# RMS norms of a two-layer prompt and decode step on one core: sums of squares by token, the inverse root spread by a product with the identity

## Chip, cores, metric

The kernel runs on one core of one Trainium2 chip, as a single launch. The metric is the device time of that launch in microseconds, the median of several runs.

## What is computed

The reference runs a trunk of two layers over 256 prompt tokens and 8 x 4 sampled tokens, 1024 features wide, all in float32. Each layer has a mixer and a feed-forward part, and each part stands between two RMS norms, so there are eight norms with 1024 features:

```python
def rms_norm(x, g):
    xf = x.astype(F32)
    y = xf * lax.rsqrt(jnp.mean(xf * xf, axis=-1, keepdims=True) + EPS)
    return (y * g.astype(F32)).astype(x.dtype)

# per layer; sh, sc, gt come from cs @ w_ada + b_ada
h = modulate(rms_norm(x, g_pre_mix), sh1, sc1)      # h * (1 + scale) + shift
x = x + gt1 * rms_norm(mixer(h), g_post_mix)
h = modulate(rms_norm(x, g_pre_ffn), sh2, sc2)
x = x + gt2 * rms_norm(ffn(h), g_post_ffn)
```

Layer 0's mixer is latent attention beside dilated attention, its feed-forward part a dense SwiGLU of width 2816. Layer 1's mixer is windowed attention with sinks, its feed-forward part eight SwiGLU experts of width 3584, two to a token.

## The kernel before, in words

All activations stand transposed: features over the 128 partitions, in eight blocks k of 128 features, and tokens along the row, 288 of them (0 to 255 prompt, 256 to 287 sampled). So `xT`, `hT`, `fT` and `sq` are each 128 x 8 x 288. PSUM has eight banks of 512 columns: `bank(i, n, at)`. Each engine has its own written-out program, and they meet at semaphores; the order of work on an engine is the order of its code. A float32 product is two passes on TensorE, and the trace has a row for each weight load and each matmul of a pass ("x2" is one product); a transpose is one pass.

Norms are numbered 0 to 7: even ones are the pre-norms, odd ones the post-norms. Each goes through four engine steps:

- Squares. ScalarE squares each block into `sq[:, k, :]`, from PSUM, from `xT` (`x_squares`) or from `fT`.
- Sums over features, in `sums(n)` of TensorE. For norm 0 and the odd norms VectorE has added the eight blocks first (`add_square`, L1864) and one product of `ones` (128 x 128, stationary) with `sq[:, 0, :]` (288 columns) gives the sums, the same on all partitions (L691). For norms 2, 4 and 6 there are eight such products, one as each block of squares arrives (L695; in `sums_and_late` L1095).
- Root: ScalarE, `std(n)`, Sqrt of 128 x 288 from bank 7 into `rstd`. Inverse: VectorE, a reciprocal of 128 x 288 from `rstd` to `rinv` in SBUF (L1849 in `pre_norm`, L1885 in `post_norm`).
- Use. `post_norm` multiplies each of eight blocks of `fT` by `rinv` (L1890) and adds it to `xT` (L1897), and each finished block releases the next norm's square. `pre_norm` multiplies the sampled tokens (L1850, L1851), then the eight blocks of the prompt (L1853), and ScalarE adds the shift to each (`add_shift`); each finished block of `hT` releases products of the next linear layer.

In layer 0 norms 1 and 2, and 3 and 4, run in `sums_and_late(n, j0)`: TensorE has three further tasks there, `late_rows` of the second layer's modulation (L1073). One task is eight blocks k of two products, each 32 stationary columns with 256 moving ones, so 32 passes. Before the change TensorE's order is: task 0, blocks 0 to 2; `sums(n)`; task 0, blocks 3 to 7; task 1, blocks 0 to 3; then the eight sums of norm n+1 with task 1's blocks 4 to 7 after sums 0, 2, 4 and 6; then the whole of task 2; then the next linear layer (L1187 feed-forward, or L1208 for the projections of layer 1). Norms 5 and 6 (layer 1) have no such tasks beside them: after norm 6 TensorE runs the router (L1238, moving operand 8 columns wide), transposes (L1246) and the counting products of the routing (L1251, L1254), then the experts. Norm 0's sums are made at the start, and its root waits until the modulation of layer 0 is ready; before its use TensorE turns the weights `kvb` (L791). Norm 7 ends the kernel: its output blocks are turned by 24 transposes (L1455) into banks 0 to 5, copied and stored.

The weight transfers are issued by SyncE in a fixed order, each as soon as the products that used its ring slot are done.

Of the kernel before, what the change touches and what calls it, by code (L numbers as in the profile page):

```python
# [18 lines left out]
ALU = mybir.AluOpType  # L19
ACT = mybir.ActivationFunctionType  # L20
AX_X = mybir.AxisListType.X

D, P, KD = 1024, 128, 8
NTP, NB, TS = 256, 8, 4
NS = NB * TS
NT = NTP + NS
# [33 lines left out]
C_EPS = C_CM + 128  # L60
# [111 lines left out]
def build(nc, t_in, t_out):  # L172
# [12 lines left out]
    with ctx:  # L185
        def sb(name, shape, dt=F32):
            return ctx.enter_context(nc.sbuf_tensor(name, shape, dt))

        def sem(name):
            return ctx.enter_context(nc.semaphore(name))  # L190
# [4 lines left out]
        xT = sb("xT", [P, KD, NT])  # L195
# [2 lines left out]
        o_or_q = sb("o_or_q", [P, KD * NT])  # L198
        rinv_rstd = sb("rinv_rstd", [P, 2 * NT])
        rinv, rstd = rinv_rstd[:, 0:NT], rinv_rstd[:, NT:2 * NT]  # L200
        mod = sb("mod", [P, 2, 48, 9])
        coef = sb("coef", [P, 4, KD, 9])
        cst = sb("cst", [P, NCST])
# [17 lines left out]
        fT = work[:, 2304:4608].rearrange("p (k n) -> p k n", k=KD)  # L221
        sq = work[:, 4608:6912].rearrange("p (k n) -> p k n", k=KD)
# [74 lines left out]
        htok = [work[:, 4608:4608 + D], work[:, 4608 + D:4608 + 2 * D], o_or_q[:, 0:D]]  # L297
        pick = o_or_q[:, D:D + 3 * PICK].rearrange("p (t n) -> p t n", t=3)
        E_BANK = ((0, 1, 2, 1), (3, 1, 2, 1))
        G_BANK = (0, 1, 2)  # L300
        logit = rt[:, 0:24].rearrange("p (t n) -> p t n", t=3)
        top = rt[:, 24:48].rearrange("p (t n) -> p t n", t=3)
        topi = rt[:, 48:72].bitcast(U32).rearrange("p (t n) -> p t n", t=3)
# [16 lines left out]
        def bank(i, n=512, at_=0, rows=P):  # L320
            return ps[0:rows, 512 * i + at_:512 * i + at_ + n]

        ident = cst[:, C_ID:C_ID + 128]
        ones = cst[:, C_ONE:C_ONE + 128]
# [8 lines left out]
        sq_done, sq_added, stat_done, std_done = sem("squares_done"), sem("squares_added"), sem("sums_done"), sem("std_done")  # L333
# [22 lines left out]
        chain_v = sem("vector_chain")  # L356
# [11 lines left out]
        e_ptp, e_pcp = sem("put_transposed"), sem("put_copied")  # L368
        chain_e = sem("vector_chain_experts")

        rest_zero = sem("rest_rows_cleared")
        k_used, s_kr = sem("key_tile_used"), sem("rope_keys_loaded")
        s_new, s_ncp = sem("new_token_scores_done"), sem("new_token_scores_copied")
# [307 lines left out]
        def _(pe):  # L681
# [5 lines left out]
            def sums(n):  # L687

                if n % 2 or n == 0:
                    pe.wait_ge(sq_added, (n + 1) // 2 + 1)  # L690
                    mm(bank(7, NT), ones, sq[:, 0, :], start=True, stop=True).then_inc(stat_done, 1)  # L691
                    return
                for k in range(KD):
                    pe.wait_ge(sq_done, 8 * n + k + 1)
                    last = mm(bank(7, NT), ones, sq[:, k, :], start=(k == 0), stop=(k == KD - 1))  # L695
                last.then_inc(stat_done, 1)

            def ada_rows(w, b, before_last=None):

# [87 lines left out]
            for hp in range(4):  # L787
# [3 lines left out]
                    last = tp(bank(b, 128, 128 * q, 64), kvb[:, c, 128 * h:128 * h + 64], ident)  # L791
                last.then_inc(t_done, 1)
                nt += 1


            def sample_rows(b, x, w, width, k, nk):

# [265 lines left out]
            def late_rows(j, k0, k1):  # L1063

                if k0 == 0:
                    landed("ada1", j)
                    if j % 3 == 0:
                        pe.wait_ge(ada_add, 12 + j)
                w = chunk("ada1", j, 0, 4096).rearrange("p (k m) -> p k m", k=KD)
                r0, c0 = 64 * (j % 3 // 2), 3072 + WA * (j % 3 % 2)  # L1070
                for k in range(k0, k1):
                    for g in range(NT_ADA):
                        last = mm(ps[r0 + CB * g:r0 + CB * g + CB, c0:c0 + WA], csT[:, k, :], w[:, k, WA * g:WA * g + WA],  # L1073
                                  start=(k == 0), stop=(k == KD - 1))
                if k1 == KD:
                    last.then_inc(ada_done, 1)
# [10 lines left out]
            def sums_and_late(n, j0):  # L1087

                late_rows(j0, 0, 3)
                sums(n)  # L1090
                late_rows(j0, 3, KD)
                late_rows(j0 + 1, 0, 4)
                for k in range(KD):
                    pe.wait_ge(sq_done, 8 * (n + 1) + k + 1)
                    last = mm(bank(7, NT), ones, sq[:, k, :], start=(k == 0), stop=(k == KD - 1))  # L1095
                    if k == KD - 1:
                        last.then_inc(stat_done, 1)
                    elif k % 2 == 0:
                        late_rows(j0 + 1, 4 + k // 2, 5 + k // 2)
                late_rows(j0 + 2, 0, KD)  # L1100

            def attention0():

# [124 lines left out]
            linear_out(2, "out_c", 4, KD, oT)  # L1228
            mm(bank(3, 4), ident, ones[:, 0:4], start=True, stop=True).then_inc(e_o, 2)
            sums(5)  # L1230
            sums(6)


            for t, (t0, n) in enumerate(TILES):
# [212 lines left out]
                    pass_body(NE * p_, p_)  # L1447
            pe.wait_ge(e_add, 64 * npass + 2)
            sums(7)

            for kk in range(2):
                pe.wait_ge(x_upd, 24 + 4 * kk + 4)
                for t, (t0, n) in enumerate(TILES):
                    for k in range(4):
                        last = tp(bank(3 * kk + t, 128, 128 * k, n), xT[:, 4 * kk + k, t0:t0 + n], ident)  # L1455
                    last.then_inc(y_tp, 1)


# [1 line left out]
        def _(act):  # L1460
            def fn(out, in_, f, **kw):
                return nc.scalar.activation(out, in_, f, **kw)  # L1462
# [3 lines left out]

            def std(n):
                act.wait_ge(stat_done, n + 1)
                fn(rstd[:, :], bank(7, NT), ACT.Sqrt, scale=1.0 / D, bias=cst[:, C_EPS:C_EPS + 1]).then_inc(std_done, 1)

            def add_shift(n, l, w):

# [342 lines left out]
            for i in range(6):  # L1815
                kk, t = i // 3, i % 3
                n = TILES[t][1]
                act.wait_ge(y_tp, i + 1)
                fn(htok[t][0:n, 512 * kk:512 * kk + 512], bank(i, 512, 0, n), ACT.Copy).then_inc(y_cp, 1)


        @block.vector
        def _(dve):
# [3 lines left out]
            def link(ins):  # L1827

                nv[0] += 1
                ins.then_inc(chain_v, 1)  # L1830
                dve.wait_ge(chain_v, nv[0])
# [8 lines left out]
            def pre_norm(n, l, w):  # L1840

                sh = mod[:, l, 24 * w:24 * w + 8, :]
                if n:
                    dve.wait_ge(x_upd, 4 * n)
                else:
                    dve.wait_ge(x_cp, KD)
                link(V.tensor_tensor(sample(hT), sample(xT), per_batch(coef[:, 2 * w, :, :]), ALU.mult))
                dve.wait_ge(std_done, n + 1)
                link(V.reciprocal(rinv[:, :], rstd[:, :]))  # L1849
                link(V.tensor_tensor(sample(hT), sample(hT), sample_rinv(), ALU.mult))  # L1850
                V.tensor_tensor(sample(hT), sample(hT), per_batch(sh), ALU.add).then_inc(h_part, 1)  # L1851
                for k in range(KD):
                    V.scalar_tensor_tensor(out=hT[:, k, 0:NTP], in0=xT[:, k, 0:NTP], scalar=coef[:, 2 * w, k, 0:1],  # L1853
                                           in1=rinv[:, 0:NTP], op0=ALU.mult, op1=ALU.mult).then_inc(h_part, 1)

            def sample_rinv():
                return rinv[:, NTP:NT].rearrange("p (b t) -> p b t", t=TS).unsqueeze(1).broadcast_to([P, KD, NB, TS])

            def add_square(n, k):

# [9 lines left out]
            def post_norm(n, m, w):  # L1870

                g = coef[:, 2 * w + 1, :, :]
                for k in range(KD):
                    if m == 3:
                        dve.wait_ge(sq_done, 8 * n + k + 1)
                    else:
                        dve.wait_ge(f_cp, 8 * m + k + 1)
                    add_square(n, k)
                    V.tensor_scalar(fT[:, k, 0:NTP], fT[:, k, 0:NTP], g[:, k, 0:1], None, ALU.mult)
                    last = V.tensor_tensor(fT[:, k, NTP:NT].rearrange("p (b t) -> p b t", t=TS),  # L1880
                                           fT[:, k, NTP:NT].rearrange("p (b t) -> p b t", t=TS),
                                           g[:, k, 1:9].unsqueeze(2).broadcast_to([P, NB, TS]), ALU.mult)
                link(last)
                dve.wait_ge(std_done, n + 1)
                link(V.reciprocal(rinv[:, :], rstd[:, :]))  # L1885
                base = nv[0]

                def scaled(k):
                    nv[0] += 1
                    V.tensor_tensor(fT[:, k, :], fT[:, k, :], rinv[:, :], ALU.mult).then_inc(chain_v, 1)  # L1890

                scaled(0)
                for k in range(KD):
                    if k + 1 < KD:
                        scaled(k + 1)
                    dve.wait_ge(chain_v, base + k + 1)
                    V.tensor_tensor(xT[:, k, :], xT[:, k, :], fT[:, k, :], ALU.add).then_inc(x_upd, 1)  # L1897
# [482 lines left out]
```

## Time and profile before

| | |
|---|---|
| time, median of 3 runs | 2053.6 us |
| lowest and highest | 2045.3 and 2057.38 us |
| the profiled execution: its own time | 2053.35 us |
| its span, first to last instruction | 2051.7 us |
| mean granted TensorE clock | 0.952 |
| busy: TensorE matmuls, weight loads, VectorE, ScalarE | 1832.5, 1356.3, 418.9, 334.2 us |
| DMA | 504.36 MB, mean 246 GB/s |

The rows come from that one execution. PE is TensorE's matmuls, PEld its weight loads, DVE VectorE, ACT ScalarE, SPq the transfer queue of SyncE; times are from the span's start. The granted clock is a share of 2.4 GHz: 1.00 is that level, 0.50 is 1.2 GHz. A mean over a stretch with both levels lies between.

### The profile page before, as it was taken

The numbers are of one execution on the slowest core, as the hardware profiler recorded it, in microseconds if no ns is written. First come the engines' busy times: TensorE is split into PE (matmuls) and PEld (weight loads), VectorE is DVE, ScalarE is ACT, GpSimd is POOL, SyncE is SP. The second block draws the span as 40 slices with busy tenths as digits, with TensorE's granted clock in tenths as the row PEclk, the third lists the DMA queues.
The fourth block names the chain that finished last, engine by engine and source line by source line (L and its number), as shares of the span: only waits on it lengthen the run. The fifth ranks groups of instructions, "written<-read, shape, count | busy, mean of one in ns | idle before, by whom it ended". The sixth has DMA issues, their size and how long they took to land.

```text
span 2051.7 us, 30167 instructions
## 1 busy us (share of the span) xinstructions
PE 1832.5 (89%) x12873; PEld 1356.3 (66%) x12874; DVE 418.9 (20%) x1260; ACT 334.2 (16%) x1000; POOL 53.3 (3%) x99
## 2 busy tenths in 40 slices
PE   6799898899999998988998979899989799988874
PEld 3455565667777745767997636399965499953532
DVE  1104333340000034642101211111012111021113
ACT  2122333230000023621100101000001010010102
POOL 1002120000000000000000000000000000000000
PEclk9998999799999997988999999999999999999997
DMA  9933857354334563051785999997749977869991
GB/s 350 363 127 115 275 212 259 111 176 156 123 98 128 166 212 81 32 214 64 275 320 206 370 398 387 402 358 267 281 164 395 394 278 302 314 231 402 386 401 40
DMA packets 252027, 504.36 MB, mean 246 GB/s; under 512 B 6953, under 2 KB 65497, under 8 KB 251746
## 3 DMA queue, kind: packets, MB, share of 16 engines
q1 hardware_dynamic: 248066, 495.49, 67.0%
q0 software_dynamic: 3808, 6.61, 1.1%
q8 instruction: 123, 2.02, 0.4%
q14 instruction: 30, 0.25, 0.0%
HBM read 499.05 MB, written 3.02 MB: 245 GB/s over the span
## 4 chain that ended last, share of the span: by engine, by line
PE 72%; DMA 12%; SPq 7%; issue 4%; DVE 3%; ACT 1%; POOL 0%; DVEq 0%
PE ps L1315 15%; PE ps L1297 8%; PE ps L1187 8%; PE ps L1365 8%; PE ps L755 7%; DMA big<-in_w_moe_out 6%; SPq L585 4%; DMA big<-in_w_ada 3%; PE ps L815 3%; PE ps L1262 3%; PE ps L1208 2%; DMA big<-in_w_moe_in 2%; PE ps L704 1%; DMA big<-in_cache_b_v 1%; SPq L539 1%
## 5 line engine op out<-in xcount | busy, mean ns | idle before, releaser
L1315 PE MATMUL ps<-big 128*128 128x128 f32 (+1 forms) x2688 | 316.2, 281 | 15.5 <-issue 15.5
L1315 PEld LDWEIGHTS ps<-big 128*128 128x128 f32 x2688 | 314.9, 194 | 16.8 <-issue 16.8
L1297 PE MATMUL ps<-big 128*64 128x256 f32 x2240 | 263.3, 393 | 45.4 <-issue 35.3
L1297 PEld LDWEIGHTS ps<-big 128*64 128x64 f32 x2240 | 163.9, 142 | 134.3 <-issue 52.5
L1187 PE MATMUL ps<-work,big 128*128 128x288 f32 x704 | 171.2, 406 | 1.0 <-ACT work L1462 1.0
L1462 ACT ACTIVATE gqkv<-ps 128x144 f32<-128x144 f32 (+1 forms) x231 | 66.6, 315 | 628.5 <-PE ps L1315 307.7
L2302 DVE TENSOR_TENSOR z<-ps,gqkv 128x256 f32<-128x256 f32 x224 | 69.1, 334 | 468.9 <-ACT gqkv L1462 468.9
L1349 PE MATMUL ps<-big,z 128*64 128x512 f32 x560 | 127.7, 598 | 37.1 <-DMA big<-in_w_moe_out 35.6
L1187 PEld LDWEIGHTS ps<-work,big 128*128 128x128 f32 x704 | 133.6, 190 | 38.3 <-issue 1.5
L1365 PE MATMUL ps<-z,big 128*128 128x128 f32 (+1 forms) x1344 | 155.6, 279 | 2.3 <-issue 2.3
L1365 PEld LDWEIGHTS ps<-z,big 128*128 128x128 f32 x1344 | 155.1, 191 | 2.8 <-issue 2.8
L1462 ACT ACTIVATE z<-ps 128x288 f32<-128x288 f32 (+5 forms) x107 | 43.9, 426 | 574.7 <-PE ps L1349 158.6
L1349 PEld LDWEIGHTS ps<-big,z 128*64 128x64 f32 x560 | 37.8, 136 | 120.8 <-issue 62.3
L704 PE MATMUL ps<-big,csT 128*32 128x256 f32 x576 | 70.0, 399 | 20.2 <-DMA big<-in_w_ada 19.0
L755 PE MATMUL ps<-z,big 128*128 128x288 f32 x352 | 85.6, 406 | 1.0 <-DVE z L2181 1.0
L1462 ACT ACTIVATE big<-ps 128x384 f32<-128x384 f32 (+11 forms) x137 | 56.0, 433 | 165.8 <-PE ps L704 63.6
L755 PEld LDWEIGHTS ps<-z,big 128*128 128x128 f32 x352 | 66.8, 190 | 19.8 <-DVE z L2181 1.4
L1462 ACT ACTIVATE work<-ps 128x288 f32<-128x288 f32 (+4 forms) x104 | 38.3, 394 | 196.7 <-PE ps L755 137.5
L704 PEld LDWEIGHTS ps<-big,csT 128*32 128x32 f32 x576 | 35.5, 115 | 49.9 <-DMA big<-in_w_ada 14.8
L755 PE MATMUL ps<-o_or_q,big 128*128 128x288 f32 x256 | 65.4, 420 | 0.6 <-ACT o_or_q L1462 0.6
L815 PE MATMUL ps<-big,work 128*128 128x512 f32 (+2 forms) x160 | 62.2, 548 | 3.3 <-ACT work L1462 3.3
L2305 DVE COPY z<-ps 128x432 f32<-128x432 f32 x8 | 4.9, 608 | 291.1 <-PE ps L1365 148.1
(319 smaller groups left out, 1646.2 us busy)
## 6 DMA issues: line engine op xcount, KB each, us to landing
big<-in_w_moe_in SPq DMA_DIRECT2D x112, 2048.0 KB, 14.8
big<-in_w_moe_out SPq DMA_DIRECT2D x56, 2048.0 KB, 19.8
big<-in_w_ada SPq DMA_DIRECT2D x24, 2048.0 KB, 13.2
big<-in_w_ffd_in SPq DMA_DIRECT2D x22, 1024.0 KB, 7.6
big<-in_w_ffd_out SPq DMA_DIRECT2D x8, 1408.0 KB, 6.8
big<-in_cache_b_k SPq DMA_DIRECT2D x4, 2048.0 KB, 8.0
big<-in_cache_mla_ckv SPq DMA_DIRECT2D x64, 128.0 KB, 2.6
big<-in_cache_b_v SPq DMA_DIRECT2D x4, 2048.0 KB, 11.6
```

The costliest lines, as they stand in the source:

```text
L585: sp.dma_start(wslot(q).rearrange("p (f m) -> p f m", f=4), src).then_inc(e_in[q], 16)
L704: last = mm(ps[CB * g:CB * g + CB, 512 * b:512 * b + WA], csT[:, k, :], w[:, k, WA * g:WA * g + WA], start=(k == 0), stop=(k == KD - 1))
L755: last = mm(bank(4 + k % 2, NT), w[:, f, 128 * m:128 * m + 128], rhs[:, f, :], start=(f == 0), stop=(f == nk - 1))
L815: last = mm(bank(nz % 4, w), hT[:, k, t0:t0 + n], wt[:, k, :], start=(k == 0), stop=(k == KD - 1))
L1187: last = mm(bank(2 * (f % 2) + g, NT), w[:, g, k, 128 * fb:128 * fb + 128], hT[:, k, :], start=(k == 0), stop=(k == KD - 1))
L1262: last = mm(bank(G_BANK[k // 3], CAP, CAP * (k % 3)), htok[t][:, 128 * k:128 * k + 128], pick[:, t, 0:CAP], start=(t == 0), stop=(t == 2))
L1297: last = mm(ps[64 * a:64 * a + 64, 512 * b + 256 * g:512 * b + 256 * g + 256], hsel[:, k, 0:NARROW], w[:, k, 256 * a:256 * a + 256], start ...
L1315: last = mm(bank(b, cols, 256 * g), w[g][:, k, 128 * i:128 * i + 128], hsel[:, k, 0:cols], start=(k == 0), stop=(k == KD - 1))
L1349: last = mm(ps[64 * d:64 * d + 64, 512 * 5:512 * 6], actT[:, q, 128 * m + 64 * half:128 * m + 64 * half + 64], w[:, i, 512 * d:512 * d + 5 ...
L1365: last = mm(bank(5 + k // 3, cols, CAP * (k % 3)), w[:, i, 128 * k:128 * k + 128], act, start=(q == 0 and i == 0 and k % 3 == 0), stop=(q ...
L1462: return nc.scalar.activation(out, in_, f, **kw)
L2302: V.tensor_tensor(out, bank(b, w, 256), sil[i % 2][:, 0:w], ALU.mult).then_inc(e_act, 1)
```

## The change

The sums are made by token instead of spread over all partitions. `sq` is now the stationary operand, in three pieces of 128 tokens (from token 0, 128 and 160: the last two overlap), and one column of `ones` is moved: three products where there was one, whose results are three columns of bank 7, a token to a partition. Root and reciprocal work on 128 x 3 (`rcol`). Then `spread(n)` on TensorE makes three products: stationary a column of `rcol` repeated 128 times, moving the identity (128 columns); that puts the inverse of every token on all partitions of bank 2, columns 0 to 287. VectorE's uses (L1850, L1853, L1890) read bank 2 instead of `rinv`. In `sums_and_late` the two `spread` calls stand two blocks of late rows behind the sums they belong to: after block 4 of task 0, and after block 1 of task 2. For norm 0 `spread` stands behind the transposes of `kvb`. The last transposes go to banks 0, 1, 3, 4, 5, 6.

```diff
--- before.py
+++ after.py
@@ -198,6 +198,7 @@
         o_or_q = sb("o_or_q", [P, KD * NT])
         rinv_rstd = sb("rinv_rstd", [P, 2 * NT])
         rinv, rstd = rinv_rstd[:, 0:NT], rinv_rstd[:, NT:2 * NT]
+        rcol = sb("rcol", [P, 2, 3])
         mod = sb("mod", [P, 2, 48, 9])
         coef = sb("coef", [P, 4, KD, 9])
         cst = sb("cst", [P, NCST])
@@ -298,6 +299,7 @@
         pick = o_or_q[:, D:D + 3 * PICK].rearrange("p (t n) -> p t n", t=3)
         E_BANK = ((0, 1, 2, 1), (3, 1, 2, 1))
         G_BANK = (0, 1, 2)
+        Y_BANK = (0, 1, 3, 4, 5, 6)
         logit = rt[:, 0:24].rearrange("p (t n) -> p t n", t=3)
         top = rt[:, 24:48].rearrange("p (t n) -> p t n", t=3)
         topi = rt[:, 48:72].bitcast(U32).rearrange("p (t n) -> p t n", t=3)
@@ -368,6 +370,7 @@
         e_ptp, e_pcp = sem("put_transposed"), sem("put_copied")
         chain_e = sem("vector_chain_experts")
 
+        rc_rdy, rb_rdy = sem("inverse_root_by_token"), sem("inverse_root_spread")
         rest_zero = sem("rest_rows_cleared")
         k_used, s_kr = sem("key_tile_used"), sem("rope_keys_loaded")
         s_new, s_ncp = sem("new_token_scores_done"), sem("new_token_scores_copied")
@@ -688,12 +691,26 @@
 
                 if n % 2 or n == 0:
                     pe.wait_ge(sq_added, (n + 1) // 2 + 1)
-                    mm(bank(7, NT), ones, sq[:, 0, :], start=True, stop=True).then_inc(stat_done, 1)
+                    token_sums(0, 0, 0).then_inc(stat_done, 1)
                     return
                 for k in range(KD):
                     pe.wait_ge(sq_done, 8 * n + k + 1)
-                    last = mm(bank(7, NT), ones, sq[:, k, :], start=(k == 0), stop=(k == KD - 1))
+                    last = token_sums(k, 0, KD - 1)
                 last.then_inc(stat_done, 1)
+
+            def token_sums(k, first, end):
+
+                for t, t0 in enumerate((0, 128, 160)):
+                    last = mm(bank(7, 1, t), sq[:, k, t0:t0 + P], ones[:, 0:1], start=(k == first and t == 0), stop=(k == end),
+                              skip_group_check=True)
+                return last
+
+            def spread(n):
+
+                pe.wait_ge(rc_rdy, n + 1)
+                for t, t0 in enumerate((0, 128, 160)):
+                    last = mm(bank(2, P, t0), rcol[:, 1, t:t + 1].broadcast_to([P, P]), ident, start=True, stop=True)
+                last.then_inc(rb_rdy, 1)
 
             def ada_rows(w, b, before_last=None):
 
@@ -791,7 +808,7 @@
                     last = tp(bank(b, 128, 128 * q, 64), kvb[:, c, 128 * h:128 * h + 64], ident)
                 last.then_inc(t_done, 1)
                 nt += 1
-
+            spread(0)
 
             def sample_rows(b, x, w, width, k, nk):
 
@@ -1088,16 +1105,20 @@
 
                 late_rows(j0, 0, 3)
                 sums(n)
-                late_rows(j0, 3, KD)
+                late_rows(j0, 3, 5)
+                spread(n)
+                late_rows(j0, 5, KD)
                 late_rows(j0 + 1, 0, 4)
                 for k in range(KD):
                     pe.wait_ge(sq_done, 8 * (n + 1) + k + 1)
-                    last = mm(bank(7, NT), ones, sq[:, k, :], start=(k == 0), stop=(k == KD - 1))
+                    last = token_sums(k, 0, KD - 1)
                     if k == KD - 1:
                         last.then_inc(stat_done, 1)
                     elif k % 2 == 0:
                         late_rows(j0 + 1, 4 + k // 2, 5 + k // 2)
-                late_rows(j0 + 2, 0, KD)
+                late_rows(j0 + 2, 0, 2)
+                spread(n + 1)
+                late_rows(j0 + 2, 2, KD)
 
             def attention0():
 
@@ -1228,7 +1249,9 @@
             linear_out(2, "out_c", 4, KD, oT)
             mm(bank(3, 4), ident, ones[:, 0:4], start=True, stop=True).then_inc(e_o, 2)
             sums(5)
+            spread(5)
             sums(6)
+            spread(6)
 
 
             for t, (t0, n) in enumerate(TILES):
@@ -1447,12 +1470,13 @@
                     pass_body(NE * p_, p_)
             pe.wait_ge(e_add, 64 * npass + 2)
             sums(7)
+            spread(7)
 
             for kk in range(2):
                 pe.wait_ge(x_upd, 24 + 4 * kk + 4)
                 for t, (t0, n) in enumerate(TILES):
                     for k in range(4):
-                        last = tp(bank(3 * kk + t, 128, 128 * k, n), xT[:, 4 * kk + k, t0:t0 + n], ident)
+                        last = tp(bank(Y_BANK[3 * kk + t], 128, 128 * k, n), xT[:, 4 * kk + k, t0:t0 + n], ident)
                     last.then_inc(y_tp, 1)
 
 
@@ -1466,7 +1490,7 @@
 
             def std(n):
                 act.wait_ge(stat_done, n + 1)
-                fn(rstd[:, :], bank(7, NT), ACT.Sqrt, scale=1.0 / D, bias=cst[:, C_EPS:C_EPS + 1]).then_inc(std_done, 1)
+                fn(rcol[:, 0, :], bank(7, 3), ACT.Sqrt, scale=1.0 / D, bias=cst[:, C_EPS:C_EPS + 1]).then_inc(std_done, 1)
 
             def add_shift(n, l, w):
 
@@ -1816,7 +1840,7 @@
                 kk, t = i // 3, i % 3
                 n = TILES[t][1]
                 act.wait_ge(y_tp, i + 1)
-                fn(htok[t][0:n, 512 * kk:512 * kk + 512], bank(i, 512, 0, n), ACT.Copy).then_inc(y_cp, 1)
+                fn(htok[t][0:n, 512 * kk:512 * kk + 512], bank(Y_BANK[i], 512, 0, n), ACT.Copy).then_inc(y_cp, 1)
 
 
         @block.vector
@@ -1846,15 +1870,16 @@
                     dve.wait_ge(x_cp, KD)
                 link(V.tensor_tensor(sample(hT), sample(xT), per_batch(coef[:, 2 * w, :, :]), ALU.mult))
                 dve.wait_ge(std_done, n + 1)
-                link(V.reciprocal(rinv[:, :], rstd[:, :]))
+                V.reciprocal(rcol[:, 1, :], rcol[:, 0, :]).then_inc(rc_rdy, 1)
+                dve.wait_ge(rb_rdy, n + 1)
                 link(V.tensor_tensor(sample(hT), sample(hT), sample_rinv(), ALU.mult))
                 V.tensor_tensor(sample(hT), sample(hT), per_batch(sh), ALU.add).then_inc(h_part, 1)
                 for k in range(KD):
                     V.scalar_tensor_tensor(out=hT[:, k, 0:NTP], in0=xT[:, k, 0:NTP], scalar=coef[:, 2 * w, k, 0:1],
-                                           in1=rinv[:, 0:NTP], op0=ALU.mult, op1=ALU.mult).then_inc(h_part, 1)
+                                           in1=bank(2, NTP), op0=ALU.mult, op1=ALU.mult).then_inc(h_part, 1)
 
             def sample_rinv():
-                return rinv[:, NTP:NT].rearrange("p (b t) -> p b t", t=TS).unsqueeze(1).broadcast_to([P, KD, NB, TS])
+                return bank(2, NS, NTP).rearrange("p (b t) -> p b t", t=TS).unsqueeze(1).broadcast_to([P, KD, NB, TS])
 
             def add_square(n, k):
 
@@ -1882,12 +1907,13 @@
                                            g[:, k, 1:9].unsqueeze(2).broadcast_to([P, NB, TS]), ALU.mult)
                 link(last)
                 dve.wait_ge(std_done, n + 1)
-                link(V.reciprocal(rinv[:, :], rstd[:, :]))
+                V.reciprocal(rcol[:, 1, :], rcol[:, 0, :]).then_inc(rc_rdy, 1)
+                dve.wait_ge(rb_rdy, n + 1)
                 base = nv[0]
 
                 def scaled(k):
                     nv[0] += 1
-                    V.tensor_tensor(fT[:, k, :], fT[:, k, :], rinv[:, :], ALU.mult).then_inc(chain_v, 1)
+                    V.tensor_tensor(fT[:, k, :], fT[:, k, :], bank(2, NT), ALU.mult).then_inc(chain_v, 1)
 
                 scaled(0)
                 for k in range(KD):
```


## Rows read from the trace of the kernel before

**Rows 1.** The page, parts 1 and 2: busy time; granted clock by slices

```profile
...
PE 1832.5 (89%) x12873; PEld 1356.3 (66%) x12874; DVE 418.9 (20%) x1260; ACT 334.2 (16%) x1000; POOL 53.3 (3%) x99
...
PEclk9998999799999997988999999999999999999997
...
```

**Rows 2.** Chain of waits, 430 to 470 us: start us, us, what

```profile
...
441.34 0.70 PE ps L691 x2
...
442.06 0.51 ACT rinv_rstd L1462
...
442.66 1.96 DVE rinv_rstd L1885
...
446.37 0.75 PE ps L1095 x2
447.13 0.56 PE ps L1073 x4
447.68 1.17 PE ps L1095 x4
...
454.17 1.97 DVE rinv_rstd L1849
...
456.16 0.44 DVE work L1850
...
458.13 11.88 PE ps L1187 x48
...
```

**Rows 3.** Timeline, 430 to 460 us (start, us, engine, line): TensorE's runs of L1073

```profile
...
441.95 4.08 PE L1073 MATMUL ps<-big,csT 128*32 128x256 f32 x36
...
```

**Rows 4.** Windows: busy us of each engine, then granted clock, DMA share, GB/s

```profile
...
446.00:454.00 8.00, 7.66 (x40) 3.54 (x40) 5.06 (x14) 3.79 (x9) 0.00 (x0) 1.00 1.00 321
...
906.00:914.00 8.00, 7.19 (x16) 4.86 (x16) 5.17 (x14) 3.76 (x9) 0.00 (x0) 0.58 0.89 326
...
918.00:926.00 8.00, 7.84 (x48) 7.81 (x48) 6.36 (x15) 2.90 (x8) 0.00 (x0) 0.50 0.00 0
...
```

**Rows 5.** Timeline, 885 to 935 us: layer 1's norms and the router

```profile
...
906.48 7.19 PE L695 MATMUL ps<-work,cst 128*128 128x288 f32 x16 [4.35 <-ACT work L1462]
...
918.16 7.95 PE L1238 MATMUL ps<-wrout,work 128*128 128x8 f32 x48 [4.50 <-ACT work L1462]
...
931.00 1.40 PE L1251 MATMUL ps<-big,cst 128*128 128x8 f32 x12
...
933.10 0.21 ACT L1462 ACTIVATE big<-big 128x3 f32<-128x3 f32 x1
...
933.54 0.18 DVE L2243 RECIPROCAL big<-big 128x3 f32<-128x3 f32 x1
...
```

**Rows 6.** Timeline of TensorE, 368 to 400 us: products of 128 columns

```profile
...
381.89 0.79 PE L1034 MATMUL ps<-big,z 128*128 128x128 f32 x2 [0.58 <-ACT big L1462]
...
382.90 0.63 PE L1036 MATMUL ps<-big,z 128*128 128x128 f32 x2
...
398.19 0.49 PE L1034 MATMUL ps<-big,z 128*128 128x128 f32 x2
...
398.74 0.39 PE L1036 MATMUL ps<-big,z 128*128 128x128 f32 x2
...
```

**Rows 7.** Groups of VectorE by form, whole span: busy us, mean ns | idle

```profile
...
L2313 DVE TENSOR_TENSOR work<-ps,work 128x288 f32<-128x288 f32 x64 | 27.0, 454 | 7.1 <-PE ps L1395 4.5 <-PE ps L1393 0.8
...
L1890 DVE TENSOR_TENSOR work<-work,rinv_rstd 128x288 f32<-128x288 f32 x32 | 14.2, 453 | 0.1
...
L1849 DVE RECIPROCAL rinv_rstd<-rinv_rstd 128x288 f32<-128x288 f32 x4 | 7.8, 1954 | 9.3 <-ACT rinv_rstd L1462 9.3
...
```

**Rows 8.** Timeline, 86 to 104 us, around norm 0

```profile
...
88.45 1.91 PE L791 MATMUL ps<-cst,big 128*64 128x128 f32 x16 [0.52 <-DVE mod L1952]
...
89.72 1.95 DVE L1849 RECIPROCAL rinv_rstd<-rinv_rstd 128x288 f32<-128x288 f32 x1
...
```

**Rows 9.** Timeline, 2018 to 2051 us, norm 7

```profile
...
2026.52 1.30 PE L691 MATMUL ps<-work,cst 128*128 128x288 f32 x2 [7.83 <-DVE work L1864]
...
```

## Prediction

> **What bounds the kernel now.** I read the page first: TensorE's matmuls are busy 1832.5 us, 89% of the span, VectorE 20%, ScalarE 16%, and the clock digits are mostly 9 [rows 1]. So a microsecond counts where TensorE waits for a norm, or where a norm's own products stand in TensorE's way. Then the chain of waits around norms 1 and 2. Norm 1's sum starts at 441.34; the reciprocal of 128 x 288 lasts 1.96 us; TensorE takes up norm 2's sums at 446.37, the second reciprocal starts at 454.17, its result is used at 456.16, and the feed-forward products start at 458.13 [rows 2]. The chain has two characters. From 446.37 to 453.5 it lies wholly on TensorE, which alternates two sums (1.17) and one block of late rows (0.56): here TensorE's throughput is the bound, not the squares. Before and behind that, root, reciprocal and hops are the bound, while TensorE works off late rows, 36 passes in 4.08, 0.113 each [rows 3]; that leaves it idle for 0.34 before the first sum, and the 32 passes behind the last one end 1.0 before the feed-forward starts. Last the clock: in 446 to 454 TensorE has 1.00; in 906 to 914, after the idle time behind norm 5, it has 0.58 though busy for 7.19 of 8.00; and in 918 to 926, in the router, 0.50 although busy for 7.84 of 8.00 [rows 4].
>
> **The change part by part.** Prices first. Root of 128 x 3: 0.21, as the small ScalarE row; reciprocal of 128 x 3: 0.18; hops 0.04 to 0.10. A token sum is three weight loads of 128 x 128 in each of two passes, with one moving column: its nearest rows are L1251, six such products with 8 columns in 1.40, and the router, 24 products in 7.95 at the low clock, 16 of them 128 tokens wide and 8 of them 32 [rows 5]. L1251 gives 0.70 for three with their end; I take 0.66 in a stream and 0.80 alone. The router gives 0.33 a product if the narrow ones cost as much as the wide ones and 0.50 if they cost nothing, so 1.0 to 1.5 for three; I take 1.33, twice the full-clock value. A spread is three products with 128 moving columns: three such in a row span 398.19 to 399.13, 0.94, at full clock and 381.89 to 383.53, 1.64, at low clock [rows 6]. VectorE's 68 uses (4 of L1850, 32 each of L1853 and L1890) now read PSUM: 454 ns with a PSUM operand against 453 without [rows 7], so nothing; for L1853's form no row shows PSUM, and I bound it by 0 and by 0.02 each.
>
> A rule speaks against token sums, too. The Trainium skill, "TensorE: Matmul & The Clock Gate", section "LDWEIGHTS (loading the stationary operand)", gives a load as its columns over 1.2 GHz whatever the contraction: 107 ns for 128, an estimate of 0.64 for a token sum, and it names no slower clock. By it the router's loads would take 3.9 us; the row has 7.84 busy [rows 4], so the trace disagrees at the low clock. The sum would be near 2059 by that rule.
>
> Norm 1. Before: sum to first use 441.3 to 444.65, 3.35 us, with a root of 0.51 [rows 2]. After: sum 0.80, root 0.21, reciprocal 0.18, hops 0.25: ready at 442.7. TensorE has meanwhile taken two blocks of late rows (8 passes, 0.87) and comes to `spread` at 442.95, so the new wait on it costs nothing; use at 443.95, 0.7 earlier. That is worth nothing by itself: the squares come 0.7 earlier, but TensorE now has 0.9 more to do before it can take them, and its idle 0.34 is all that hides it. It starts the sums at 446.9 instead of 446.37. The loop of eight sums: a period was 1.17 + 0.56 = 1.73; now 2 x 0.66 + 0.43 (four passes of late rows) + 0.2 for the switches = 1.95. Loop 8.0 instead of 7.2. At full clock norm 2's sum is ready at 454.85, 1.3 late; root to use costs 1.8 (late-row blocks and spread included) instead of 2.6, so use 0.55 late; and TensorE, with spread among its 32 late passes, is free for the feed-forward at 459.3 instead of 458.13. So **+1.2** at full clock.
>
> But I don't expect full clock. In that loop 5.3 of 8.0 us would be weight loads with one column moved. The only stretch of such work in the trace, the router, kept 0.50 for all its 8 us with TensorE busy, and the clock came back only in the 128-column transposes behind it; the sums of 906 to 914, 288 columns wide, won it back within their own 7.2 us [rows 4, 5]. So the loop should lose the clock in its middle. With some 2.9 us of it left, that costs 2.9; the two late blocks 0.9 and the spread 0.7 more; of the 24 late passes behind it (2.7 us at full clock) I let a few run slow, 0.5 more, since wide work runs again from the end of the loop on. +1.2 + 2.9 + 0.9 + 0.7 + 0.5 = +6.2, taken as **+6**. Bounds: +1.2 with the clock kept, +10 if it is lost early in the loop and not back when the feed-forward starts. Norms 3 and 4 have the same code around them and, by the timeline, the same times to 0.1 us: **+6** again. The feed-forward and projection products behind them are TensorE's own throughput, so nothing takes it back; the weight transfers wait for slots that these free, and shift along.
>
> Norms 5 and 6. First use 0.9 earlier (3.4 less 2.45), no late rows. Sums of norm 6 from 905.6, at the low clock as now, 8 x 1.33 = 10.6 instead of 7.19: their end comes at 916.2, not 913.7. Root to use 2.4 with a low-clock spread (2.6 before): **+2.3**, and the router behind it is at the low clock in both. Nothing follows it but a chain of small steps, all of it shifted.
>
> Norm 0: TensorE is through L791 at 90.36; a spread of 0.94 gives 91.4, the reciprocal's end was 91.67 [rows 8]: **-0.3**. Norm 7, at the low clock: the sum took 1.30 [rows 9], now 1.45; root and reciprocal save 0.3 and 1.77, spread and a hop add 1.74: **-0.2**. New banks at the end, no new wait: 0.
>
> Sum: 6 + 6 + 2.3 - 0.3 - 0.2 = +13.8, against the profiled execution's own 2053.35 (span 2051.7 and 1.65 around it): 2067.2. That execution lies 0.25 below the median shown, so the same holds for the median. Since the clock may come back sooner in one of the pairs, I say 2066.
>
> **Rivals.** *The clock holds in both loops.* For it: the late rows between the sums, 256 columns, are no weight loads, and they had 1.00 among the wide sums. Against: the router. The time is 1.2 + 1.2 + 2.3 - 0.5 = +4.2, 2057.5: not slower by what a measurement can tell. The Trainium skill, same page, section "Part 1: The HAM clock gate (the \"warmup\" mystery)", says the gate goes by how busy the engine has recently been; by that rule the loop, busy throughout, would hold. The router, busy 7.84 of 8.00 at 0.50, contradicts it.
>
> *The spread fills norm 5's pause.* 0.94 us of products in the 5 us between norm 5's sum and norm 6's might keep the clock up. Then a token sum (0.66) keeps pace with the squares, which come a use and an add of VectorE apart (0.45 busy each, overlapping [rows 7]), norm 6 is used 3.6 earlier, and the router and what follows gain some 1.5 more. With held loops: 2.4 - 5.1 - 0.5 = -3.2, 2050. It decides only if the clock is still 1.00 at 905.6; in the rows of before it is 0.50 by 906, and one short burst is little against a pause of over 3 us. Faster by over 0.5% I can't build from any case.
>
> *The clock stays away longer.* If the low stretch reaches through both loops' tails into the linear layers, 10 each: +22, 2075.
>
> *It doesn't do what it says*: VectorE slower on PSUM or a reciprocal of three columns with a long fixed part. The rows above leave 2 us at most.
>
> **How the numbers follow.** 0.5% is 10.3 us, about what a measurement of this kernel can tell from no change (the three runs shown lie within 12 us). Forecast 0.62, clock held in the loops 0.22, spread fills the pause 0.06, clock away longer 0.10. The forecast lies 3 us above the bound, and one loop's bounds reach below it, so a fifth of it counts as no change. Slower 0.62 x 0.8 + 0.10 = 0.60; same 0.12 + 0.22 + 0.03 = 0.37; faster 0.03. Range: 2054 to 2076, from just under the held clock to the longer loss; the forecast alone 2061 to 2072.
>
> **What would show it.** Right: granted clock clearly under 1.00 in some part of 446 to 462 and of 723 to 739; the last sum of norms 2 and 4 four microseconds late; feed-forward and projections starting about 6 late; norm 6's sums lasting over 10 us; the uses of L1890 0.37 apart as before. Wrong: clock 1.00 through both loops, or norm 6's sums as fast as the squares arrive.

## The result and the profile after

The changed kernel takes 2058.94 us (median of 20 runs) where the kernel before takes 2052.35 (20 runs on the same chip): ratio 1.0033, 95% interval 1.0017 to 1.005, so +7 us, with an interval from +3 to +10. The profiled execution itself took 2050.91 us, less than the profiled one of before (2053.35): the two spans alone would call the change faster. So I read the stages, not the spans. (One of the 20 runs of the changed kernel, 2234.75 us at a mean granted clock of 0.813, is left out of the ratio, as are the two runs like it in the experiments, 2446.88 and 6385.98 us.)

The chain of waits of the changed kernel through norms 1 and 2, the counterpart of [rows 2] (start in us, length, engine, what, line, instructions); L704 is a pass of a token sum (x6 is one token sum: three products of two passes), L712 of a spread, L1090 of late rows, L1208 the feed-forward:

```profile
439.96 0.22 PE ps L704 x2
440.19 0.56 PE ps L1090 x4
440.74 1.43 PE ps L704 x12
442.17 0.87 PE ps L1090 x4
443.04 2.65 PE ps L704 x12
445.69 0.99 PE ps L1090 x4
446.68 1.37 PE ps L704 x6
448.05 1.85 PE ps L1090 x8
449.90 1.58 PE ps L712 x6
451.48 3.24 PE ps L1090 x24
454.72 15.47 PE ps L1208 x63
```

Two token sums (x12) take 1.43 in the first rows and 2.65 in the fifth; late rows go from 0.56 to 0.99. Nothing waits: the chain is TensorE's from end to end, where before it went over ScalarE and VectorE. Root and reciprocal have left it, and the clock has taken more than they gave. The windows say so [rows 4]: granted clock (the figure third from the end) of 1.00, then a mean of 0.77 and of 0.64, with TensorE busy throughout.

```profile
431.00:438.00 7.00, 7.00 (x62) 4.16 (x56) 4.67 (x14) 3.14 (x7) 0.00 (x0) 1.00 0.99 318
438.00:446.00 8.00, 8.00 (x52) 6.20 (x54) 2.71 (x8) 1.89 (x5) 0.00 (x0) 0.77 0.78 249
446.00:455.00 9.00, 9.00 (x50) 5.03 (x47) 3.62 (x10) 2.44 (x7) 0.00 (x0) 0.64 0.74 233
```

The changed kernel's chain of waits through norms 5 and 6, the counterpart of [rows 5]:

```profile
900.52 0.84 PE ps L704 x6
901.39 0.27 ACT rcol L1486
901.71 0.04 issue
901.76 0.19 DVE rcol L1910
901.94 0.04 issue
901.99 0.95 PE ps L712 x6
902.96 0.82 DVE work L1916 x2
...
904.68 10.41 PE ps L704 x48
915.11 0.27 ACT rcol L1486
...
915.70 1.67 PE ps L712 x6
917.39 0.43 DVE work L1875
```

Norm 5, at full clock, goes from sum to use in 2.44 us (900.52 to 902.96). The eight token sums of norm 6 take 10.41 at the low clock (granted 0.50 from 904.7 to 915.1), where eight wide sums took 7.19 [rows 5]. And the changed kernel's groups of VectorE by form, the counterpart of [rows 7]: reading the inverse from PSUM costs nothing (before, from SBUF: 453 ns for the first form and 477 for the second).

```profile
L1916 DVE TENSOR_TENSOR work<-work,ps 128x288 f32<-128x288 f32 x32 | 13.9, 446 | 5.4 <-PE ps L712 5.4
L1878 DVE SCALAR_TENSOR_TENSOR work<-xT,coef,ps 128x256 f32<-128x256 f32 x32 | 12.9, 474 | 0.0
```

To compare many profiles I cut each into stretches, from the start of one named pass to the start of another (differences of starts in the trace, us). "Norm 0": first transpose of `kvb` to first projection. "Pair 1" and "pair 2": last pass of the output projection (of the feed-forward) to the first pass of the next layer's products. "Norms 5, 6": last pass of layer 1's output projection to the router. "Experts": first gathering product to last combining one; "sixth": the sixth expert of them. "Norm 7": from there to the first output transpose. In brackets: time at half clock. Stages are read from one execution per row. The rows of the experiments below stand here too.

| kernel, profile | norm 0 | attention 0 | pair 1 | pair 2 | attention 1 | norms 5, 6 | experts | sixth | norm 7 |
|---|---|---|---|---|---|---|---|---|---|
| before | 5.22 | 345.8 (44) | 18.62 | 18.61 | 165.0 (38) | 18.49 (8.9) | 1081.3 | 174.8 | 15.62 |
| before, again | 5.22 | 346.0 (44) | 18.61 | 18.61 | 163.0 (31) | 16.96 (3.9) | 1082.7 | 174.7 | 15.61 |
| changed | 4.58 | 336.7 (21) | 24.79 (10) | 24.84 (10) | 161.4 (31) | 20.43 (16) | 1078.5 | 170.7 | 15.40 |
| changed, again | 4.58 | 355.3 (72) | 26.34 (14) | 24.85 (10) | 161.4 (31) | 20.44 (16) | 1075.4 | 170.7 | 15.40 |
| changed, third | 4.58 | 343.0 (34) | 24.79 (10) | 24.84 (10) | 161.4 (31) | 20.44 (16) | 1075.3 | 170.4 | 15.40 |
| 128 columns moved | 4.57 | 344.0 (44) | 20.74 (0) | 20.74 (0) | 164.9 (38) | 16.46 (4.1) | 1076.7 | 170.6 | 15.60 |
| pairs as before | 4.57 | 343.3 (38) | 18.62 | 18.61 | 165.0 (38) | 20.44 (15) | 1076.2 | 170.7 | 15.39 |
| mixed | 4.57 | 346.1 (44) | 19.27 (0) | 24.13 (10) | 160.6 (27) | 17.14 (9.3) | 1078.3 | 171.4 | 15.39 |
| pairs as before, 128 columns | 4.58 | 341.6 (41) | 18.61 | 18.61 | 165.1 (38) | 16.68 (3.8) | 1077.2 | 170.5 | 15.61 |
| before + 34 products | 5.22 | 350.4 (54) | 18.61 | 18.61 | 164.0 (34) | 18.18 (9.2) | 1075.4 | 170.5 | 15.61 |
| before + 82 products | 5.22 | 344.8 (41) | 18.61 | 18.61 | 161.4 (31) | 17.72 (6.8) | 1078.3 | 170.7 | 15.61 |
| before + 82, again | 5.22 | 342.4 (34) | 18.61 | 18.61 | 165.1 (38) | 18.41 (9.0) | 1075.6 | 170.5 | 15.63 |

The first three rows already hold the puzzle. Around the norms the changed kernel loses 6.2 + 6.2 + 1.9 and gains 0.6 + 0.2: +13.5, the forecast's +13.8. But the time moved by half of that, +7 us.

### The profile page after: what moved, and what is told of

Same layout as the page of the kernel before. It is cut to its first block, busy times and chain, and to the rows that moved or that the text cites. A ratio compares the mean times of both kernels' runs of the same rounds, so it can differ in the third digit from the quotient of the medians.

```text
span 2049.3 us, 30495 instructions
## 1 busy us (share of the span) xinstructions
PE 1841.4 (90%) x13037; PEld 1376.5 (67%) x13038; DVE 404.2 (20%) x1260; ACT 332.3 (16%) x1000; POOL 53.4 (3%) x99
## 4 chain that ended last, share of the span: by engine, by line
PE 75%; DMA 11%; SPq 6%; issue 4%; DVE 2%; ACT 1%; POOL 0%; DVEq 0%
PE ps L1338 15%; PE ps L1320 9%; PE ps L1208 8%; PE ps L1388 8%; PE ps L772 7%; DMA big<-in_w_moe_out 6%; SPq L588 4%; DMA big<-in_w_ada 3%; PE ps L832 3%; PE ps L1285 3%; PE ps L1229 2%; PE ps L721 2%; PE ps L704 1%; PE ps L1090 1%; DMA big<-in_cache_b_v 1%
## 5 line engine op out<-in xcount | busy, mean ns | idle before, releaser
L1338 PEld LDWEIGHTS ps<-big 128*128 128x128 f32 x2688 | 314.7, 194 | 13.5 <-issue 13.5
L1208 PE MATMUL ps<-work,big 128*128 128x288 f32 x704 | 171.3, 406 | 0.0
L1208 PEld LDWEIGHTS ps<-work,big 128*128 128x128 f32 x704 | 133.6, 190 | 37.2 <-issue 0.4
## 6 DMA issues: line engine op xcount, KB each, us to landing
big<-in_w_ada SPq DMA_DIRECT2D x24, 2048.0 KB, 13.5
```

The costliest lines, as they stand in the source:

```text
L1208: last = mm(bank(2 * (f % 2) + g, NT), w[:, g, k, 128 * fb:128 * fb + 128], hT[:, k, :], start=(k == 0), stop=(k == KD - 1))
L1338: last = mm(bank(b, cols, 256 * g), w[g][:, k, 128 * i:128 * i + 128], hsel[:, k, 0:cols], start=(k == 0), stop=(k == KD - 1))
```

## Experiments

I had three theories at first. A: the remainder is chance in attention, where the time at half clock wanders. B: the new kernel gains something behind the norms. C: the loops lose the clock by accident.

**1. Both kernels once more.** No edit.

> The kernel before once more, for the spread of its stages. Theory A (the loops of sums cost what was forecast, and the stages whose code is the same in both kernels differ by chance): from norm 1's sum to the feed-forward 16.9 us again and from norm 3's to the projections 16.9, to 0.1; but the two attention stages, 345.8 and 165.0 us in the first profile, move by several us, with the time at half clock. Theory B (the new kernel gains something in the stages behind the norms, in attention or among the experts): those stages repeat within 1 us here, at 345.8, 165.0 and 1081.

> The changed kernel once more. Theory A: both loops lose the clock again, the two stretches cost 5 to 7 us more than before's 16.9 each, and the attention stages lie anywhere between the values of the two first profiles. Theory B: attention again near 336.7 and 161.4, experts near 1078.5. Theory C (the loss of clock is an accident of that profile, not of the loop): at least one of the two loops runs at 1.00 here and costs 1 to 2 us.

Measured: 2051.3 and 2067.43 us, one run each. The table shows A's wandering in the changed kernel: attention 0 from 336.7 to 355.3, in step with its time at half clock (21 to 72 us). These 18.6 us cover the 16.5 between its two executions (2050.91 and 2067.43). In the kernel before attention 0 did not move (345.8 and 346.0), against what A expected there; attention 1 moved by 2.0. C is out: both loops are again at half clock for part of their time, at +7.7 and +6.2 us, the first above the 5 to 7 expected. But the experts repeat, within each kernel and not across: the sixth takes 174.8 and 174.7 before and 170.7 twice after. That is B's kind of finding.

**2. The same sums with 128 columns moved.**

```diff
-    last = mm(bank(7, 1, t), sq[:, k, t0:t0 + P], ones[:, 0:1], ...)
+    last = mm(bank(7, 128, 128 * t), sq[:, k, t0:t0 + P], ones[:, 0:128], ...)
...
-    fn(rcol[:, 0, :], bank(7, 3), ACT.Sqrt, ...)
+    fn(rcol[:, 0, :], bank(7, 384).rearrange("p (t n) -> p t n", n=128)[:, :, 0], ACT.Sqrt, ...)
```

> The sums by token move 128 columns of ones instead of one (three blocks of 128 equal columns in bank 7, the root reads one of each); nothing else differs from the changed kernel. If what takes the clock away is that weight loads with one moving column leave the array without work (A), both loops keep 1.00 and cost 1 to 2 us instead of 6 (a load of 128 columns and 128 moving columns are equally long, so a token sum stays at 0.65), norm 6's sums win the clock back after some us and end 1 to 3 us sooner, and the time is 10 us under the changed kernel's, 2 to 4 over the kernel before. If the clock falls for another reason (C), loops stay at 23 us and the time stays the changed kernel's.

Measured: ratio to before 0.9967 (0.9945 to 0.9989), 2044.77 us. Both loops stay at 1.00, and the pairs take 20.74 us instead of 24.8: 128 times the columns moved, done 4 us sooner. Where two token sums took 2.65 us in the changed kernel's chain above, no two of them take more than 1.53 in the chain of waits of this one:

```profile
445.40 0.56 PE ps L1090 x4
445.96 1.53 PE ps L704 x12
447.49 0.56 PE ps L1090 x4
448.05 1.53 PE ps L704 x12
449.58 0.56 PE ps L1090 x4
450.14 1.53 PE ps L704 x12
451.67 0.56 PE ps L1090 x4
```

And in the same kernel's chain of waits norm 6's sums, 7.05 instead of 10.41, with the root behind them:

```profile
907.13 7.05 PE ps L704 x48
914.21 0.27 ACT rcol L1486
```

So what takes the clock away in the loops is shown: the weight loads, their number and the waits are the same in both kernels, and TensorE is busy throughout in both; only the columns moved behind each load differ (and, with them, how the root reads bank 7). The price at full clock is somewhat more than forecast: 2.13 a pair, not 1 to 2. Norm 6's sums ended 3.4 us sooner, not 1 to 3. The time, however, came out 7 below the kernel before, where I had expected 2 to 4 above it. That is again the unexplained gain.

**3. The pairs put back.** A set `BY_TOKEN = (0, 5, 6, 7)`; norms outside it take the old products, root, reciprocal and `rinv`.

```diff
+            def one_sum(n, k, first, end):
+                if n in BY_TOKEN:
+                    return token_sums(k, first, end)
+                return mm(bank(7, NT), ones, sq[:, k, :], start=(k == first), stop=(k == end))
...
             def spread(n):
+                if n not in BY_TOKEN:
+                    return
```

> Norms 1 to 4 as before, norms 0, 5, 6 and 7 as in the change. A: both loops at 16.9 us and 1.00; the rest as in the changed kernel: -0.6 at norm 0, +1.9 at norms 5 and 6, -0.4 at norm 7, so +1 us against the kernel before. B: -6, because the gain behind the norms stays without the loops' cost.

Measured: 0.9965 (0.9943 to 0.9987), 2044.24 us: B's number. Pairs 18.6 as before; norms 0, 5, 6 and 7 as in the changed kernel, by the table some +1 us together; the sixth expert at 170.7. The gain sits in code that no edit touches. Timeline of TensorE at the sixth expert's start, before (start, us, line, passes, idle before it):

```profile
1629.53 3.11 PE L1315 MATMUL ps<-big 128*128 128x128 f32 x13 [6.58 <-issue]
1635.34 9.93 PE L1315 MATMUL ps<-big 128*128 128x128 f32 x72 [2.70 <-issue]
```

and in the changed kernel:

```profile
1632.97 12.29 PE L1338 MATMUL ps<-big 128*128 128x128 f32 x91 [6.58 <-issue]
```

Each expert starts with a branch on its token count. At seven of the eight TensorE then stands on "issue", that is on nothing that the profile shows: 5.8 to 7.4 us in the first profile of before, 6.58 at the sixth. Before, it runs 13 passes and stands again for 2.70, at the same pass in both profiles (2.64 in the second); after, it runs through. Behind the second pause the clock also comes back later: 10.2 us at half clock in that expert instead of 6.8. Together 4.1 us. That made theory D: it is a matter of where the instructions lie, since the change adds 328 of them on TensorE (30167 to 30495 in the page's first line), 308 ahead of the experts and 20 in norm 7, behind them. E: it has to do with when the experts start, or with what the norms leave behind.

**4. The kernel before, with instructions added that do nothing.**

```diff
             sums(0)
+            for _ in range(34):          # 82 in the second kernel
+                mm(bank(6, 1, 500, 32), ident[0:32, 0:32], ones[0:32, 0:1], start=True, stop=True)
             pe.wait_ge(c_cp, 2)
```

> The kernel before with 34 tiny products (32 x 32 stationary, one column moved, never read) on TensorE in its pause before the first modulation weights: 136 more instructions, as the kernel with the old pairs had, no other difference. Theory D (the experts' 5 us come from where the code lies: TensorE stalls longer or shorter at the experts' branches as its instruction stream is shifted): norm stages at 5.2, 18.6, 18.6 as before, but the sixth expert at 170.7 instead of 174.7 and the experts' stage 5 us shorter at 1077; time 4 to 5 under the kernel before. Theory E (the gain comes from when the experts start, or from what the norms leave behind): experts at 1081 to 1083, time as before.

> The same with 82 tiny products, 328 more instructions, as many as the change adds. D: a sixth expert of 170.7, and a further stall of 5 us within the third expert's start as in the changed kernel. E: as the kernel before.

Measured: 34 products, 0.9982 (0.9963 to 1.0001), 2046.51 us: by the time alone not shown to be faster. 82 products, a single run of 2044.21 us; experiment 7 times this kernel again. Both have a sixth expert of 170.5 to 170.7 and no second pause there; the first with 34:

```profile
1632.07 13.17 PE L1317 MATMUL ps<-big 128*128 128x128 f32 x100 [6.54 <-issue]
```

D holds: nothing in the norms or in the experts was changed. E falls: the sixth expert's products start at 1627.3 and 1629.5 us where the second pause is there, and anywhere from 1624.3 to 1649.3 us in the ten profiles where it is not.

One detail of D fell: the further pause of 5 us that the changed kernel has in its third expert did not come with 82 products. The two shifts are not equal, though, as the counts ahead of the experts show: 308 instructions in the changed kernel and in the one with 128 columns, 116 in "pairs as before" and "pairs as before, 128 columns", 136 with 34 products (and in the mixed kernel of experiment 5), 328 with 82. Each shift has its own pattern, the same in all its profiles. A second pause in the third expert lasts 1.2 to 1.3 us before, 5.1 to 5.4 at 308, and there is none of over 1 us at 116, 136 and 328; at 328 the eighth expert has one of 2.4 to 2.5. So a shift does not only remove such pauses, it also makes them elsewhere.

**5. Parts of the pairs.** `BY_TOKEN = (0, 1, 4, 5, 7)`.

> Norms 0, 1, 4, 5 and 7 by token, 2, 3 and 6 as before: it parts the price of the pairs. Pair 1 then has a narrow sum and a spread for norm 1 and the old loop at full clock: its 18.6 us grow by 0.5 to 0.9 if the spread stands in TensorE's way as forecast, and the clock stays 1.00. Pair 2 has the old norm 3 and the narrow loop of norm 4: the clock falls, and the stretch grows by 4.5 to 6. Norm 5 alone by token: from norm 5's sum to the router 0.9 shorter than with both old at the same clock.

Measured: 2049.68 us. Pair 1, with norm 1 by token and the old loop, takes 19.27, +0.66, at full clock; pair 2, with the old norm 3 and the narrow loop, 24.13, +5.5, with 10 us at half clock. Chain of waits of pair 1:

```profile
440.99 0.76 PE ps L713 x6
441.75 0.99 PE ps L1101 x8
442.74 0.86 PE ps L723 x6
443.60 3.15 PE ps L1101 x28
446.75 0.68 PE ps L708 x2
```

There is no wait between these rows: the spread (L723) is 0.86 us more in a queue that had 0.34 us of idle time to give. The root and reciprocal that it made shorter were not what the queue waited for. Norm 5 by token with norm 6 as before took 17.14 from projection to router, 1.3 under the profile of before with about as long at half clock (18.49), where I had expected 0.9. The sixth expert, without the second pause but with 10 us at half clock as before, took 171.4: of the 4.1 us above, most is the pause itself.

**6. The best parts together**: pairs as before, 128 columns moved for norms 0, 5, 6 and 7.

> Norms 1 to 4 as before, norms 0, 5, 6 and 7 by token with 128 columns moved: pairs at 18.6 and 1.00, norm 0 0.6 shorter, norms 5 and 6 at 16.5 to 17, norm 7 with its end 0.4 shorter. With D 6 to 8 us under the kernel before, with E 1 to 3.

Measured: 0.9973 (0.9951 to 0.9996), 2044.21 us. By the stretches it gains 0.6 at norm 0 and some 1.3 at norms 5 and 6 over the kernels with old norms (mean of their five profiles 17.95), and keeps the 4 us of position; norm 7 gains nothing (15.61 against 15.62). It is faster than the kernel before by 5 to 6 us, just under the 6 to 8 expected, but not shown to be faster than that kernel with idle instructions added (2044.21 us against 2046.51 with 34 products and, in experiment 7, 2043.81 with 82).

**7. The changed kernel against one with equally many instructions in all**, on one chip.

> The changed kernel, timed on the same chip as the next one. By the stages (norm 0 -0.6, pairs +6.2 to +7.7 and +6.2, norms 5 and 6 +2.6, norm 7 -0.5, code position -4 to -5): 2057 to 2062, 6 to 11 over the kernel before.

> The kernel before with 328 more instructions on TensorE and no other change, so that it stands where the changed kernel's instructions stand. If position explains what my sum lacked: 2 to 5 under the kernel before, and the changed kernel 11 to 15 over this one, which is what the forecast summed (+13.8). If position does not matter here: as the kernel before, and the changed kernel 6 to 8 over it.

Measured: the changed kernel 1.0021 (0.9994 to 1.0048), 2058.16 us; the kernel before with 82 products 0.996 (0.9936 to 0.9985), 2043.81 us. The means of their 11 and 12 runs differ by 12.8 us, with 4.6 to either side, inside the 11 to 15 expected. So the norms' change by itself costs what was summed, and the kernel it was compared with held a stall that all four shifts tried here remove. Against the kernel before, however, both came out lower than I had put them: +4 us, not 6 to 11, and -8, not -2 to -5. The intervals (some 5 us to either side) reach the expected values; whether the kernel before loses 2 or 3 us more, in a place that the stages do not show, stays open.

## Why the prediction was right or wrong

- **The loop loses its clock: right, with its size.** Forecast +6 for each pair; 6.2, 6.2, 7.7, 6.2, 6.2 and 6.2 in six stretches. At full clock a period was given as 1.95; the rows have 1.43 + 0.56 = 1.99. The half-clock token sum, 1.33 by doubling 0.66, is 2.65 / 2 = 1.33, though the full-clock one is 0.72 and not 0.66. The last sum of norm 2 ends 4.1 us later than before, counted from the start of the stretch, where four was forecast. The size is in part luck: the full-clock part was put at +1.2 and is larger, 0.66 with norm 1 alone by token and 2.13 for all with 128 columns, of which some 0.4 is those columns (1.53 against 1.43 for two sums). That leaves, as an estimate, 1.7 for it and 4.5 for the clock, where the sum had 1.2 and 5.0; the two errors cancel.
- **The rival in which the clock holds, and the rule of the Trainium skill beside it: wrong.** "TensorE: Matmul & The Clock Gate", "Part 1: The HAM clock gate (the \"warmup\" mystery)", has the clock follow how busy the engine has been. TensorE was busy 8.00 of 8.00 us and 9.00 of 9.00 in the windows above, where the granted clock was 0.77 and 0.64, and 10.37 of 10.40 at 0.50 in norm 6's sums. What the profile calls busy does not tell it: experiment 2 changed only the columns.
- **The Trainium skill's price of a weight load** ("TensorE: Matmul & The Clock Gate", section "LDWEIGHTS (loading the stationary operand)"), six loads for an estimate of 0.64 us, with no slower clock named: near at full clock, where the rows have 1.43 / 2 = 0.72, and half of the truth at the low one, 1.33. The trace disagrees with it there. The 2059 that the prediction gives beside this rule stands without a working.
- **Norms 5 and 6: right.** Forecast +2.3; 20.44 against a mean of 17.95 is +2.5. Sums 10.41 us for a forecast 10.6. Against the second profile of before alone it would be +3.5: what it loses depends on when the clock comes back in the old sums.
- **Norm 0: -0.3 forecast, -0.64 measured.** The spread took 0.68 there, not 0.94. It follows the transposes without a wait, so its first load may be hidden behind them; that is not shown. **Norm 7: -0.2 and -0.2.** The root of three columns takes 0.27, not 0.21; small beside the rest. The spread does not fill norm 5's pause, as forecast: norm 5's sum and spread run at 1.00 (0.84 and 0.95 us), and norm 6's sums start at 0.50.
- **PSUM operands: right**, 446 ns against 453 before, and 474 against 477 for L1853's form.
- **What failed is the sum's last step.** "6 + 6 + 2.3 - 0.3 - 0.2 = +13.8" took every stage without an edit as unmoved. I had asked what the transfers, the queues and the banks of the experts would do, and not where their instructions would lie. The term that is missing is about -4 to -5 us, in the experts: without the second pause of 2.70 us and the half clock behind it, 4.1 less in the sixth expert, and about 1 in the seventh (108.0 and 108.4 before; 106.8 to 107.3 in the profiles of the changed kernel and of the kernel before with idle products). The rest of the gap, +13.8 less 4 to 5 against a measured +3 to +10, lies within the interval, with the open end of experiment 7. A change of +7 us was below the 0.5% that I counted as a change, and I gave that outcome 0.37, and the slower one 0.60. That 2058.94 lies in the range of 2054 to 2076 is luck: the range went down to there for the case that the clock holds, which did not come; the range of the forecast alone, 2061 to 2072, misses it.
- Nothing in the profile of before said whether the second pause of 2.70 us was a fixed cost or an accident of layout. It was visible there, as "issue" that no engine released, and the sum passed over it.

## What to carry to other kernels

Turning a product round so that its data are stationary and one column moves makes it a matter of weight loads: price it by rows of weight loads, at both clock levels. Here such products brought TensorE to half clock for 10 us in and behind each loop, though it did not wait there; 128 columns moved behind each load kept 1.00 and cost next to nothing (1.53 us against 1.43 for two sums). Even so the pairs stayed 2.13 us slower than before. Work that shortens a chain through other engines gains nothing where TensorE's own queue is the bound, and what it adds to that queue is paid in full. For effects under 0.5% compare stage by stage, and against more than one kernel with idle instructions added: the shift of code behind the edit moved the time by a third of what the edit did.

## What the runs showed that I had not expected

Adding 34 products that do nothing to the kernel before takes 4.3 us off an expert that starts 1.6 ms later (174.8 to 170.5), and with 82 of them the whole kernel is 0.4% faster (0.996, 0.9936 to 0.9985). The pause begins 3 us after TensorE has set out on the expert behind the branch. In the trace's instruction queue a block of 16384 bytes is issued at 1632.8 us in the kernel before, just after the second pause begins (1632.6). It arrives at 1633.9, and TensorE goes on at 1635.3, 1.4 us later. In the changed kernel the block at the corresponding place is issued at 1636.2, and TensorE doesn't stop for it. All pauses on "issue" of over 1 us at the experts' starts, first and second ones, in all twelve profiles, end in this way: 1.3 to 1.7 us after such a block has arrived. That TensorE had run out of instructions there is how I read it, and these times support it; I tried no experiment on it beyond shifting the code.

The third expert takes 113.0 us with the further pause of 5 us and without. What TensorE waits for from 1221 to 1336 us, the third expert's stretch, says why (us in total, times, longest), before:

```profile
PE ps L1297 <- issue: 7.7, 2, 6.4
PE ps L1297 <- DMA big<-in_w_moe_in: 4.5, 3, 1.8
```

and in the changed kernel, where no wait for `in_w_moe_in` is left:

```profile
PE ps L1320 <- issue: 11.6, 2, 6.3
```

The pause falls where TensorE would have waited for weights. In the sixth expert it waits for no weights in either kernel, and there the pause is paid in full.
